# Decoder layer step: key loads for the decode scores by eight samples and sixteen key chunks, with the scores turned into rows through DRAM

## The reference, cut to what matters

```python
ATT_GROUPS = ((128, 1), (512, 4), (2048, 16))      # (window, dilation), 4 heads of 128 each
def dilated_attn_decode(q, k_all, v_all, buf_len, dil, n_back):     # n_back = 128
    idx = buf_len + jnp.arange(S)[:, None] - jnp.arange(n_back + 1)[None, :] * dil
    kg, vg = k_all[:, idxc], v_all[:, idxc]
    s = jnp.einsum('bshe,bsjhe->bhsj', q, kg, ...) * ATT_SCALE
    p, lse = masked_softmax_lse(s, valid[None, None])
    o = jnp.einsum('bhsj,bsjhe->bshe', p, vg)
```

## Time and profile before

| what | value |
|---|---|
| median of 3 runs | 2077.59 us (2077.44 to 2078.93) |
| the profiled execution, its own time | 2081.41 us |
| span of its instructions | 2079.6 us |
| PE busy | 2066.8 us, 99% |
| DVE, ACT, POOL busy | 65%, 47%, 22% |
| mean granted TensorE clock | 0.999 |
| transfers | 526.47 MB, mean 253 GB/s |

### The profile page before, as it was taken

How to read it: one execution, slowest core, us unless ns; L and a number is a source line. 1 busy time by engine, 2 the same in 40 slices (tenths; PEclk the granted TensorE clock), 3 DMA queues, 4 the chain that set the end, 5 groups by cost and what they waited for, 6 DMA issues and landing times.

```text
span 2079.6 us, 48839 instructions
## 1 busy us (share of the span) xinstructions
PE 2066.8 (99%) x19331; PEld 2050.3 (99%) x19331; DVE 1343.4 (65%) x1449; ACT 986.7 (47%) x1189; POOL 449.4 (22%) x510
## 2 busy tenths in 40 slices
PE   9999999999999999999999999999999999999999
PEld 9999999999999999999999999999999999999999
DVE  7567567775555767766768968665555555555555
ACT  6654344444444545654454365554443444434443
POOL 0686414420000206763304430110000000000000
PEclk9999999999999999999999999999999999999999
DMA  8987789997897788759959976679887888878974
GB/s 252 275 276 226 260 260 270 279 264 260 251 266 221 234 299 277 236 179 321 329 177 326 283 229 196 193 248 279 263 260 244 254 271 265 260 244 256 268 217 159
DMA packets 442478, 526.47 MB, mean 253 GB/s; under 512 B 41520, under 2 KB 423392, under 8 KB 439552
## 3 DMA queue, kind: packets, MB, share of 16 engines
q1 hardware_dynamic: 427184, 507.59, 78.7%
q0 software_dynamic: 3248, 11.62, 1.6%
q10 hardware_dynamic: 11936, 5.72, 1.4%
HBM read 506.75 MB, written 105.04 MB: 294 GB/s over the span
## 4 chain that ended last, share of the span: by engine, by line
PE 92%; DVE 3%; DMA 3%; POOL 1%; ACT 1%; issue 1%; SPq 0%; ACTq 0%; DVEq 0%; POOLq 0%
PE pa L1551 30%; PE pa L1556 29%; PE pa L1552 29%; DMA qb<-q_dram 2%; DVE w_lo L1063 1%; PE pb L1754 0%; DMA raw<-in_w_in 0%; DVE xg_lo L1080 0%; DMA raw<-in_ffn_w_up 0%; PE pb L1862 0%; PE pb L1892 0%; POOL silu_v L2175 0%; DMA out_kv_p<-k_rows 0%; ACT w_hi L665 0%; PE pa L1920 0%
## 5 line engine op out<-in xcount | busy, mean ns | idle before, releaser
L1063 DVE TENSOR_TENSOR w_lo<-raw,w_hi 128x1024 fp32r<-128x1024 f32 x735 | 930.5, 1279 | 510.5 <-ACT w_hi L665 505.7
L665 ACT ACTIVATE w_hi<-raw 128x1024 fp32r<-128x1024 f32 x735 | 767.1, 1054 | 664.1 <-PE pa L1556 552.1
L1551 PE MATMUL pa<-xg_hi,w_hi 128*128 128x264 f32 x3960 | 924.6, 278 | 0.0
L1552 PE MATMUL pa<-xg_lo,w_hi 128*128 128x264 f32 x3960 | 916.2, 276 | 0.0
L1551 PEld LDWEIGHTS pa<-xg_hi,w_hi 128*128 128x128 f32 x3960 | 748.4, 189 | 8.3 <-issue 6.3
L1552 PEld LDWEIGHTS pa<-xg_lo,w_hi 128*128 128x128 f32 x3960 | 748.6, 189 | 0.2
L1556 PE MATMUL pa<-xg_hi,w_lo 128*128 128x264 f32 x3960 | 526.5, 276 | 0.0
L1556 PEld LDWEIGHTS pa<-xg_hi,w_lo 128*128 128x128 f32 x3960 | 483.3, 189 | 0.0
L1551 PE MATMUL pa<-act_hi,w_hi 128*128 128x264 f32 x1632 | 378.4, 276 | 0.0
L1552 PE MATMUL pa<-act_lo,w_hi 128*128 128x264 f32 x1632 | 377.9, 276 | 0.0
L1552 PEld LDWEIGHTS pa<-act_lo,w_hi 128*128 128x128 f32 x1632 | 308.5, 189 | 0.0
(11 more groups left out here) (364 smaller groups left out, 1353.3 us busy)
## 6 DMA issues: line engine op xcount, KB each, us to landing
raw<-in_ffn_w_up SPq DMA_DIRECT2D x172, 512.0 KB, 6.3
raw<-in_ffn_w_gate SPq DMA_DIRECT2D x171, 512.0 KB, 5.1
out_kv_s<-in_cache_kv_w SPq DMA_DIRECT2D x165, 512.0 KB
raw<-in_ffn_w_down SPq DMA_DIRECT2D x160, 512.0 KB, 4.6
raw<-in_w_in SPq DMA_DIRECT2D x152, 512.0 KB, 5.6
raw<-in_w_out SPq DMA_DIRECT2D x32, 512.0 KB, 4.9
raw<-in_w_ssm_branch SPq DMA_DIRECT2D x16, 512.0 KB, 4.6
raw<-in_ffn_w_down SPq DMA_DIRECT2D x16, 384.0 KB, 4.0
```

The lines of the kernel that those rows point to most:

```text
L665: act.activation(w_hi[:, slot], raw[:, slot], ACT.Copy).then_inc(hi_ready, 1)
L1063: dve.tensor_tensor(w_lo[:, slot], raw[:, slot], w_hi[:, slot].bitcast(f32), ALU.subtract).then_inc(lo_ready, 1)
L1551: pe.matmul(out, wh, in_order(hi), start=first, stop=False)
L1552: pe.matmul(out, wh, in_order(lo), start=False, stop=False)
```

## The change

A unit is now (g, key), with `KEYS` = 8: the load of unit n brings, for all 8 samples, every eighth key of group g. The partition is 16 x sample + chunk, where chunk c holds the keys 8c to 8c + 7. The repeated queries are thus the same for all 8 units of a group (partition 16b + c holds sample b's query), so three loads of them do for all, one into each `qb`, behind units 0, 6 and 14. `sc_dec` is laid out by head slot, group and key. The scores no longer pass through PE: ACT stores `sc_dec` to a new DRAM tensor `sc_dram` at (3, 2), after the last sum, waits for that store at (4, 0), and issues four loads (one for each head slot) into `dec_p`. DVE copies the three columns of the new keys from `pb` into `dec_p`, waits for the loads, and takes the maximum from `dec_p`; ACT's exponential works in `dec_p`. PE's three transposes and its wait for `sc_ready` go.

```diff
@@ -178,6 +178,7 @@
     top = [16512]
+    KEYS = 8
@@ -288,7 +289,7 @@
     x_fin = tile("x_fin", [P, 2, NTILE])
-    sc_dec = tile("sc_dec", [P, NG, NS, NSLOT])
+    sc_dec = tile("sc_dec", [P, NSLOT, NG, KEYS])
     kq = tile("kq", [P, NG, NS, NSLOT])
@@ -304,6 +305,7 @@
     x_dram = nc.dram_tensor("x_dram", [P, KD * T], f32).ap()
+    sc_dram = nc.dram_tensor("sc_dram", [NSLOT, NG, NS, P], f32).ap()
     y_dram = nc.dram_tensor("y_dram", [2, SC, P // 2, 4 * (NS + NB)], f32).ap()
@@ -342,7 +344,7 @@
         "prod_ready sc_ready kq_ready ds_done dmax_ready dexp_ready dec_step diag_ready dt_done dec_ready")
-    pv_done, pv_read = sems("pv_done pv_read")
+    pv_done, pv_read, sc_stored, sc_loaded = sems("pv_done pv_read sc_stored sc_loaded")
@@ -385,7 +387,7 @@
     UNIT_LOAD, UNIT_USE = 17, 13
-    UNITS = [(g, b) for g in range(NG) for b in range(NS)]
+    UNITS = [(g, key) for g in range(NG) for key in range(KEYS)]
     E0, M0 = TB_E, TB_M
@@ -527,7 +529,7 @@
                             n = v_slab - UNIT_LOAD
-                            g, b = UNITS[n]
+                            g, key = UNITS[n]
                             if n == 0:
@@ -535,11 +537,12 @@
                             dil = GROUPS[g][1]
-                            src = caches[g][b, 0].rearrange("(m r) h d -> m r (h d)", r=dil)[:, 0, :]
+                            src = caches[g][:, 0].rearrange("b (c k r) h d -> b c k r (h d)", k=KEYS, r=dil)[:, :, key, 0, :]
                             sync.dma_start(ku[n % 4][:], src).then_inc(ku_loaded[n % 4], 16)
-                            if n >= 3:
-                                sync.wait_ge(prod_ready, n - 2)
-                            sync.dma_start(qb[n % 3][:], q_dram[g * NS + b:g * NS + b + 1, :].to_broadcast([P, 512])).then_inc(qb_loaded[n % 3], 16)
+                            if n in (0, 6, 14):
+                                q = (0, 6, 14).index(n)
+                                sync.dma_start(qb[q][:],
+                                               q_dram[q * NS:q * NS + NS, None, :].to_broadcast([NS, P // NS, 512])).then_inc(qb_loaded[q], 16)
             while tails:
@@ -881,9 +884,18 @@
                     act.activation(halves(att_hi[:, 0:3])[:, :, :, H0], by_parity(att_v[:, 0:3, 0:NT]), ACT.Copy).then_inc(att_hi_ready, 1)
+                if i == 3 and j == 2:
+                    act.wait_ge(sc_ready, len(UNITS))
+                    act.dma_start(sc_dram.rearrange("h g b (c k) -> (b c) (h g) k", k=KEYS),
+                                  sc_dec[:].rearrange("p h g k -> p (h g) k")).then_inc(sc_stored, 16)
+                if i == 4 and j == 0:
+                    act.wait_ge(sc_stored, 16)
+                    for hh in range(NSLOT):
+                        act.dma_start(dec_p[hh:NS * NSLOT:NSLOT, 0:NG * P].rearrange("b (g m) -> b g m", g=NG),
+                                      sc_dram[hh].rearrange("g b m -> b g m")).then_inc(sc_loaded, 16)
                 if i == 5 and j == 0:
                     act.wait_ge(dmax_ready, 1)
-                    act.activation(dec_p[:], pb[0:32, 3, 0:NG * P + NG], ACT.Exp, bias=stat[0:32, 9:10], scale=SCALE,
+                    act.activation(dec_p[:], dec_p[:], ACT.Exp, bias=stat[0:32, 9:10], scale=SCALE,
                                    accum_out=stat[0:32, 10:11]).then_inc(dexp_ready, 1)
@@ -1297,7 +1309,9 @@
                     dve.wait_ge(ds_done, 1)
-                    dstep(dve.tensor_reduce(stat[0:32, 8:9], pb[0:32, 3, 0:n + NG], AX.X, ALU.max))
+                    dstep(dve.tensor_copy(dec_p[:, n:n + NG], pb[0:32, 3, n:n + NG]))
+                    dve.wait_ge(sc_loaded, 16 * NSLOT)
+                    dstep(dve.tensor_reduce(stat[0:32, 8:9], dec_p[:], AX.X, ALU.max))
                     dve.tensor_scalar(stat[0:32, 9:10], stat[0:32, 8:9], -SCALE, None, ALU.mult).then_inc(dmax_ready, 1)
@@ -1458,9 +1472,9 @@
                         if 0 <= n < len(UNITS):
-                            g, b = UNITS[n]
+                            g, key = UNITS[n]
                             dve.wait_ge(prod_ready, n + 1)
-                            dve.tensor_reduce(sc_dec[:, g, b, :], prod[n % 2][:], AX.X, ALU.add).then_inc(sc_ready, 1)
+                            dve.tensor_reduce(sc_dec[:, :, g, key], prod[n % 2][:], AX.X, ALU.add).then_inc(sc_ready, 1)
                         if j == 3 and name == "u":
@@ -1817,11 +1831,8 @@
                 if (i, j) == (4, 2):
-                    pe.wait_ge(sc_ready, len(UNITS))
                     pe.wait_ge(kq_ready, 1)
                     pe.wait_ge(att_read, 2)
-                    for g in range(NG):
-                        pe.transpose(pb[0:32, 3, g * P:(g + 1) * P], sc_dec[:, g].rearrange("p b h -> p (b h)"), ident[:])
                     for g in range(NG):
@@ -2191,10 +2202,11 @@
                 pool.wait_ge(ku_loaded[n % 4], 16 * (n // 4 + 1))
-                pool.wait_ge(qb_loaded[n % 3], 16 * (n // 3 + 1))
+                g = UNITS[n][0]
+                pool.wait_ge(qb_loaded[g], 16)
                 if n >= 2:
                     pool.wait_ge(sc_ready, n - 1)
-                pool.tensor_tensor(prod[n % 2][:].rearrange("p h d -> p (h d)"), ku[n % 4][:], qb[n % 3][:], ALU.mult).then_inc(prod_ready, 1)
+                pool.tensor_tensor(prod[n % 2][:].rearrange("p h d -> p (h d)"), ku[n % 4][:], qb[g][:], ALU.mult).then_inc(prod_ready, 1)
```

## The result

| | median us | lowest to highest | runs |
|---|---|---|---|
| before | 2077.44 | 2076.45 to 2078.93 | 7 |
| after | 2085.39 | 2082.56 to 2087.54 | 7 |

The ratio is 1.0038, with a 95% interval from 1.0029 to 1.0048: the change costs 7.95 us. The forecast of 2076.4 us, its range up to 2081.8 and its likeliest outcome (no difference that can be told) were all wrong. The profiled execution of after took 2086.78 us, with a span of 2085.0.

A forecast was written before the change was run, and what follows sets the result against it. PE's own work was taken as the bound (busy 2066.8 of 2079.6 us). Slabs -0.8, transposes -0.4 and new waits 0 gave -1.2 us, from the median 2077.59 to 2076.4 us; range 2074.5 to 2081.8.

The forecast's parts named there:

- The key loads: Key loads of the decode scores: same bytes and 2 KB runs from 8 samples, costed as before, so no change.
- Rival B: Key loads sit on 8 engines, doubling their share there: -0.4 to +4.2 us, taken as 2079.5 us; chance 0.35.
- a pace of 3.33: In the decode scores, SP starts one unit's loads every 3.33 us; busy engines were to need 3.08 us a unit.
- Rival C: Slow key reads at large address steps in the last 8 or 16 units: +2.2 to +12.5, 2084.6 us; chance 0.07.
- The query loads: 21 of 24 query loads go, weight slabs land sooner, and 0.8 us of PE's 1.23 us loss returns.
- The transposes: Three PE transposes at (4, 2) go, covered by nothing: -0.4 us.
- ACT and DVE: New store, four loads, waits and copy: store 5 us, issues 1.7 us, loads out at 1037.8; cost nothing.
- the cover of 9.55 us: Time ACT's split of slab (5, 0) had to spare before PE wants it; it was to move about 0.8 us.
- D: Scores' way through DRAM takes over 16 us, so DVE and ACT's split come late: +6, 2083.6 us; chance 0.03.
- Key loads that land no sooner than 7 us while the GB/s fall: Sign in the changed profile that key loads sit on 8 engines, beside a PE still waiting near 1030 us.
- PE waiting over 2 us in a new place: Sign that the forecast is wrong: PE waits more than 2 us somewhere it did not before.
- ACT's wait for the store: Sign for the forecast: ACT's wait at (4, 0) for the scores' store should be under 2 us.

The follow-up runs named there:

- x9: The after kernel with each unit's keys read from one sample's cache and 16 outermost at the key load's source: 2078.27 us, ratio 1.0003.
- x4: The after kernel with each unit's keys read from one sample's cache, 8 still outermost at the key load's source: 2084.26 us, ratio 1.0038.
- x3: The before kernel with its key load's source in two dimensions, 16 outermost, same rows in another order: 2096.63 us, ratio 1.0093.
- x8: The before kernel with the key load's source replaced by eight rows repeated 16 times, 16 outermost: 2094.69 us, ratio 1.0077.
- x1_again: The after kernel with partitions numbered 8 x chunk + sample, 16 chunks outermost, same addresses; second set of runs: 2077.81 us, ratio 1.0003.
- x12: The before kernel with only three query loads in place of one a unit, keys unchanged: 2078.06 us, ratio 1.0002.
- x5: The after kernel without the scores' store, loads and waits through DRAM, PE's three transposes back: 2085.99 us, ratio 1.0036.
- before again: The before kernel, unchanged, run and profiled a second time: 2077.4 us in 8 runs, ratio 1.0004.
- x6: The after kernel with its three query loads each repeating one row, so spread over 16 engines; keys unchanged: 2084.99 us, ratio 1.0034.
- x2: The before kernel with its key load's source in two dimensions, 8 outermost, one query load a unit kept: 2103.23 us, ratio 1.0126.
- x11: The after kernel with each unit's keys read from one sample's cache and 4 outermost at the source: 2115.27 us, ratio 1.0173.

## Why the prediction was wrong

**The key loads** are the step of the prediction that failed: "They bring as many bytes in as many runs of 2 KB, from 8 samples in place of one. I cost them as before". I costed the bytes and the addresses and not the shape. The shape costs twice: the load sits on half the engines (x9 against x4, and the packets in flight), and the form in two parts lengthens packets, its own and the slabs' (x3, x8). Against the 61.04 us of an undisturbed stretch, after's distance of 69.19 is 8.15 too long. This term is +8.15 and not 0. x1_again is the cleanest neighbour: its (0, 0) starts at 979.80, after's at 979.74, and the spans are 2076.9 and 2085.0 us, 8.1 apart.

**Rival B** was the right mechanism, and I had it at 2079.5 and at most 4.2 us slower. Its price was too small because I gave the busy engines 1.54 us for a key load, twice 0.77, hence "exactly as before", 3.08 a unit against a pace of 3.33. That had no room for a second effect, and the pace is now 3.59:

```profile
L541 SPq DMA_DIRECT2D ku<-in_cache_kv_w x24: 607/619/2121, 943.6 to 1026.2; - x24
```

(1026.2 - 943.6) / 23 = 3.59. If the busy engines set it, a key load takes them at most 3.59 - 1.54 = 2.05 us, 1.33 times what I gave it; the queues' 1.5 times, worked out above, would be 2.4 and does not quite fit, so the exact price on 8 engines stays open. Rival C held the arithmetic of just this case: once B holds, it decides from 1.16 times on and brings 2.2 to 12.5 us. I tied it to slow addresses, which x4 refutes, and gave it 0.07. What I left out was a load that is slow, and slows others, by its form.

**The query loads.** The bytes went as forecast (x12: slabs 5.5, share near 0.75). But "of the 1.23 us between 0 and all can return. I take 0.8" took a wait of one execution for a property of the kernel. The prediction itself notes that this execution lies 3.8 us above the median, and carries its gain over to the median all the same. The second profile has no such wait: the term is 0 there, and no median shows a gain.

**The transposes** gave 0.32 of the 0.4 forecast. **ACT and DVE** were right in their result: the store took 4.8 us where 5 was taken, the loads were out at 1044.5 and DVE did not wait. The four issues took twice the 1.7 us of the estimate, which had been read from SP's queue, and the cover of 9.55 us hid that. D is refuted by x5.

The sum with these sizes is +8.15 + 0 - 0.32 + 0 = +7.83 us; measured are 7.95. That they agree so closely is in part luck: the 8.15 is of one execution, 1.4 us above after's median, and other executions with 8 outermost had less (x4 66.68 - 61.04 = 5.64, near its own median).

**Signs.** "Key loads that land no sooner than 7 us while the GB/s fall" could not be read, since after's profile has no landing for them, nor has that of any kernel here with 8 or 4 outermost. The slabs of 8.4 us, at falling GB/s, said it in their place. POOL waited for keys for 50.5 us, which the prediction had at little. The sign of being wrong, PE waiting over 2 us in a new place, came true at (1, 2) with 2.64. ACT's wait for the store, forecast at under 2 us, was nothing.

**How late is too late?** Three slabs of 2.7 us are made ahead, 8.1 us, as the prediction has it. Median landings of 5.5, 6.3 and 7.7 us cost PE nothing (x12, before again, x1_again), 8.4 costs 8.15 us and 10.6 costs 17.2 (x3: distance 978.61 to 1056.85, 78.24, some of it the clock's, which was 0.96 there from 960 to 1040). But x5, with a median of 7.7 like x1_again's, lost 4.3 us. The slowest slab tells them apart: here is the landing of `raw` from 940 to 1020, first in x1_again, then in x5_pe_rows, then in after.

```profile
DMA to landing us min/median/max: 4.2/7.7/8.5
```

```profile
DMA to landing us min/median/max: 4.6/7.7/10.6
```

```profile
DMA to landing us min/median/max: 4.5/8.4/11.8
```

Over all profiles the order holds: where the slowest slab took up to 8.9 us (x12 7.2, x1_again 8.5, before again 8.9) nothing was lost, at 9.6 (x9) 1.1 us, from 10.1 to 10.9 (x6, x5, x4) 4.3 to 5.6, at 11.8 (after) 8.15, and at 12.1 to 13.1 (x3, x8, x2, x11) 15.4 to 24.7. The first profile of before falls out of the order, with 10.5 us and 1.4 lost.

No version here beats the kernel before. The change with 16 outermost has 21 loads and three transposes less and the same time.

## What to carry to other kernels

Cost a DMA by its shape as well as by its bytes: what stands outermost at the source and which partitions it fills decide how many engines carry it and, here, how long its packets and those beside it take, and when a dimension such as "samples" moves to the front, try the other order of the partitions first. A mean DMA share under 1 with falling GB/s and later landings of the other loads was here the mark of a transfer that sits on part of the engines. And before a wait of 1 us becomes a term of a sum, see whether the profiled execution lies above the median: what it has too much is no gain to be had.

## What was unexpected of the hardware

- A 256 KB load into 128 partitions whose source has 16 outermost and 8 within cost about 1.5 us of all 16 engines in four kernels, where one with 128 rows in a single dimension cost 0.79: same bytes, same runs of 2 KB, and in x3_before_16 the same rows. Packets of 2 KB took 119 to 124 ns in the mean and not 96, and the 1 KB packets beside them 59 to 64 and not 51. That alone made the kernel before 19 us slower.
- The same transfers on 16, 8 and 4 engines, in an otherwise equal kernel: 2078.27, 2084.26 and 2115.27 us. By the Trainium skill, DMA: Bandwidth & Descriptors, on why a DMA increments its semaphore by 16, the number of engines is the largest up to 16 that divides the outermost dimension of both sides; the three times agree with it, and so do the packets in flight (8 or 9 for 19% of the time with 8 outermost, 4 or 5 for 31.7% with 4).
- The same page, on latency and other measured facts, has half the rate for copies between DRAM tensors of 128 rows of 16 KB that lie 4 or 8 MB apart, against rows 512 KB apart. No run here has such copies. For these loads of 2 KB rows, samples up to 8 MB apart (the last group) or one sample's keys make no difference, with 8 outermost (2085.39 and 2084.26) or with 16 (2077.81 and 2078.27).
- Four issues of 12 KB loads on ACT's queue took 3.44 us, 0.67 to 1.20 each.
